# Where the gate weights of a piece stand among its w2 loads, and the gate units in front of the w2 steps, in the last stages of a one-layer Hymba-style kernel

## The reference

```
xn = RMSNorm(x);  z = xn @ W_in                       # RG-LRU heads and attention heads, then W_out, residual
h  = h + HierMoE(RMSNorm(h))                          # top group of 4, top 2 of its 8 experts, 32 experts in all
         expert e: (silu(t @ w1[e]) * (t @ w3[e])) @ w2[e],  w1, w3: 2048 x 512,  w2: 512 x 2048
pe   = RMSNorm(p @ W_ple)
gate = sigmoid(RMSNorm(h) @ w_pg + b_pg)              # w_pg: 2048 x 2048
out  = h + gate * pe
```

## Time and profile before

| | us |
|---|---|
| median of 3 runs (lowest, highest) | 1387.04 (1386.98, 1390.51) |
| the profiled execution | 1388.14 |
| its span, first to last instruction | 1386.1 |
| TensorE busy in the span | 1089.3 (79%) |
| mean granted TensorE clock | 0.900 of full |

### The profile page before, as it was taken

The page is one execution under the profiler, slowest core; times in us unless marked ns, Lnnn a source line. Parts: engine busy times, 40 slices in busy tenths (PEclk is TensorE's granted clock), DMA queues, the critical chain, the costliest instruction groups (busy, mean ns, idle before and its releaser), DMA issues.

```text
span 1386.1 us, 13825 instructions
## 1 busy us (share of the span) xinstructions
PE 1089.3 (79%) x6016; PEld 504.8 (36%) x6016; DVE 285.3 (21%) x439; ACT 156.7 (11%) x314; POOL 53.4 (4%) x66
## 2 busy tenths in 40 slices
PE   8999999999876686666765667666576656989998
PEld 4458887445522232222222223222232212333333
DVE  1104726412321212121221121000000000111116
ACT  1111315002200011000000000000000000010102
POOL 0112110200000002000000000000000000000000
PEclk9999999999888899788898788888888877999999
DMA  9943334354599999999999999999999999999961
GB/s 351 305 152 122 122 122 147 129 217 182 227 426 426 429 426 427 429 426 428 429 426 428 428 426 426 415 427 428 414 427 415 427 428 409 384 395 387 397 267 61
DMA packets 91053, 476.14 MB, mean 344 GB/s; under 512 B 10272, under 2 KB 10416, under 8 KB 67952
## 3 DMA queue, kind: packets, MB, share of 16 engines
q1 hardware_dynamic: 84896, 471.88, 84.1%
q0 software_dynamic: 560, 2.88, 0.6%
q10 hardware_dynamic: 5536, 0.47, 0.3%
HBM read 473.12 MB, written 2.10 MB: 343 GB/s over the span
## 4 chain that ended last, share of the span: by engine, by line
DMA 50%; PE 47%; SPq 1%; DVE 1%; issue 1%; ACT 0%; DVEq 0%
DMA ring<-in_w 48%; PE ps L1421 8%; PE ps L1384 6%; PE ps L1851 6%; PE ps L1674 5%; PE ps L1754 4%; PE ps L1545 4%; PE ps L1558 4%; PE ps L1809 2%; DMA area<-in_w 2%; PE ps L1646 2%; PE ps L1822 1%; PE ps L1639 1%; SPq L386 1%; PE ps L1578 1%
## 5 line engine op out<-in xcount | busy, mean ns | idle before, releaser
L1754 PE MATMUL ps<-ring,area 128*32 128x512 f32 x1024 | 166.4, 796 | 122.6 <-DMA ring<-in_w 122.0
L1674 PE MATMUL ps<-ring,area 128*32 128x512 f32 x976 | 147.7, 724 | 126.2 <-DMA ring<-in_w 126.2
L1184 DVE TENSOR_TENSOR h<-ps,h 128x2048 f32<-128x2048 f32 x32 | 73.3, 2292 | 298.8 <-PE ps L1646 298.8
L1754 PEld LDWEIGHTS ps<-ring,area 128*32 128x32 f32 x1024 | 43.1, 139 | 232.3 <-issue 232.3
L1421 PE MATMUL ps<-hT,ring 128*128 128x256 f32 x512 | 112.9, 380 | 0.0
L1674 PEld LDWEIGHTS ps<-ring,area 128*32 128x32 f32 x976 | 31.6, 122 | 222.7 <-issue 222.4
L1421 PEld LDWEIGHTS ps<-hT,ring 128*128 128x128 f32 x512 | 96.5, 190 | 14.0 <-issue 1.2
L1851 PE MATMUL ps<-ring,area 128*128 128x512 f32 x192 | 88.6, 603 | 6.3 <-DMA ring<-in_w_pg 4.9
L1384 PE MATMUL ps<-ring,hT 128*128 128x512 f32 x192 | 85.0, 602 | 1.1 <-DVE hT L907 1.1
L1229 DVE TENSOR_TENSOR hT<-area,ps 128x128 f32<-128x128 f32 x16 | 4.6, 288 | 315.8 <-ACT area L860 315.8
L1639 PE MATMUL ps<-area,hs 128*128 128x128 f32 x512 | 66.2, 284 | 0.5 <-DVE area L1165 0.5
(11 more groups left out here) (278 smaller groups left out, 775.0 us busy)
## 6 DMA issues: line engine op xcount, KB each, us to landing
ring<-in_w SPq DMA_DIRECT2D x157, 2048.0 KB, 21.5
ring<-in_w SPq DMA_DIRECT2D x57, 1024.0 KB, 15.1
ring<-in_w_in SPq DMA_DIRECT2D x28, 1024.0 KB, 12.6
ring<-in_w_out SPq DMA_DIRECT2D x16, 1024.0 KB, 7.2
ring<-in_w_pg SPq DMA_DIRECT2D x12, 1024.0 KB, 15.7
area<-in_w SPq DMA_DIRECT2D x2, 2048.0 KB, 14.0
hs<-in_w SPq DMA_DIRECT2D x4, 1024.0 KB, 14.3
hs<-in_w_pg SPq DMA_DIRECT2D x3, 1024.0 KB, 17.4
```

The source lines that it names most:

```text
L1184: dve.tensor_tensor(h[:, t, :], ps[:, bank:bank + 4, :].rearrange("p b n -> p (b n)"), h[:, t, :], ALU.add).then_inc(acc_done, 1)
L1674: ins = mm(ps[SLOTS * g:SLOTS * g + SLOTS, 0, :], XG[:, b, k, SLOTS * e:SLOTS * e + SLOTS], s[:, D_EXP * kk:D_EXP * kk + D_EXP], start=(k ...
L1754: ins = mm(ps[SLOTS * g:SLOTS * g + SLOTS, 0, :], XG[:, b, k, SLOTS * e:SLOTS * e + SLOTS], s[:, D_EXP * kk:D_EXP * kk + D_EXP], start=(k ...
```

## The change

The four `w_pg` chunks of piece i are loaded in front of the last quad of w2 of the same piece i (piece 0's stand first of all, piece 3's last of all, as before). In each of the three stages two gate units of the piece before stand in front of each w2 step, so that all eight are done in front of the last w2 step. VectorE adds all eight in front of `add_piece`. The counts of used chunks follow the new order.

```diff
 def w2_used(i, q, k):
     if i == 0:
         return QUAD_CHUNKS * q + 4 * W13_CHUNKS + k + 1
-    return OPEN_CHUNKS + 20 * (i - 1) + 4 * q + k + 1
+    behind_gate = 4 if q == OPEN_QUADS - 1 else 0
+    return OPEN_CHUNKS + (4 * OPEN_QUADS + 4) * (i - 1) + 4 * q + behind_gate + k + 1
 def w_pg_used(i, kk):
-    return OPEN_CHUNKS + 20 * i + 16 + kk + 1
+    return OPEN_CHUNKS + (4 * OPEN_QUADS + 4) * i + 4 * (OPEN_QUADS - 1) + kk + 1
+def gate_units(q):
+    return range(-(-8 * q // OPEN_QUADS), -(-8 * (q + 1) // OPEN_QUADS))
 def piece_loads():
-    order = []
+    order = [("w_pg", 0, kk, 0) for kk in range(4)]
     for i in range(1, PIECES):
         w2_ = [("w2", i, q, k) for q in range(OPEN_QUADS) for k in range(4)]
-        w_pg_ = [("w_pg", i - 1, kk, 0) for kk in range(4)]
-        order += w_pg_ + w2_ if i == 1 else w2_[:4] + w_pg_ + w2_[4:]
-    return order + [("w_pg", PIECES - 1, kk, 0) for kk in range(4)]
+        w_pg_ = [("w_pg", i, kk, 0) for kk in range(4)]
+        order += w2_ + w_pg_ if i == PIECES - 1 else w2_[:-4] + w_pg_ + w2_[-4:]
+    return order
...
             for i in range(PIECES):
                 if i:
-                    for u in range(7):
+                    for u in range(2 * 4):
                         add_gate(i - 1, u)
                 add_piece(i)
-                if i:
-                    add_gate(i - 1, 7)
                 copy_turned(i)
...
             for i in range(1, PIECES):
                 for q in range(OPEN_QUADS):
-                    if i > 1:
-                        w2_piece(i, q)
-                        if q:
-                            scatter_piece(i, q - 1)
-                    gate_unit(i - 1, 2 * q)
-                    if q < OPEN_QUADS - 1:
-                        gate_unit(i - 1, 2 * q + 1)
-                    if i == 1:
-                        w2_piece(i, q)
-                        if q:
-                            scatter_piece(i, q - 1)
+                    for u in gate_units(q):
+                        gate_unit(i - 1, u)
+                    w2_piece(i, q)
+                    if q:
+                        scatter_piece(i, q - 1)
                 scatter_piece(i, OPEN_QUADS - 1)
-                gate_unit(i - 1, 7)
                 turn_piece(i)
```

## The result

The changed kernel takes 1391.49 us (median of 22 runs, 1390.25 to 1397.27) against 1388.97 of the kernel before (22 runs, 1385.93 to 1390.98). The ratio is 1.0028, with an interval of 1.0019 to 1.0037: a quarter of a per cent slower, or 3.9 us. It weighs all executions and isn't the quotient of the two medians, which is 1.0018. Fifteen of the 22 times lie between 1390.2 and 1391.9, two at 1393.7 and 1393.9, and five between 1396.0 and 1397.3. The profiled execution, 1397.27 us with a span of 1394.9, is the slowest of the 22, which will matter.

A forecast was written before the change was run, and what follows sets the result against it. The piece stages were read as a race between a full load stream and TensorE, nearly balanced. Piece 3's units at 1353.0 against 1352.0, plus 2.5 clock, less 0.3 tail: +3.2, taken as +3.0; median 1390.0 us, range 1385.0 to 1394.5.

The forecast's parts named there:

- The late last quad: Piece 1's last w2 quad: loads 21 to 24 land 10 us later than before, at 1237.4; scatters end at 1243.6.
- The hand-off: Last scatter to next piece's gate units: adds and turn no longer covered, 3.56 us at each of three hand-offs.
- Start of piece 1's units: First gate unit of piece 1: 1243.6 plus a hand-off of 3.56, so it starts at 1247.2.
- No load is late behind it: Behind piece 1's last quad: all load waits go, 6.8 + 2.5 us; load 44 is 0.3 late at worst.
- The clock at hand-offs: Behind the three bare hand-offs: half of three clock falls of 1.7 us each, 2.5 us; ends 0 and 5.1.
- rival A: The clock falls at every hand-off: 1.0 + 5.1 = +6 us, 1393, slower; chance 0.27.
- the row of piece 0: Profile row of the kernel before: clock fell to 0.50 behind piece 0's turn for 3.3 us; evidence for falls.
- The sum: Whole span: 1353.0 + 2.5 - 1352.0 - 0.3 = +3.2, taken as +3.0 us; median 1390.0 us, 0.22% more.
- The terms without falls: The sum's part without clock loss at hand-offs: piece 3's units at 1353.0 against 1352.0, and 0.3 off the tail.
- The bound below: Were w2 (1, 3) not late, load 44 sets piece 2's units at 1298.8, piece 3's at 1351.7: -0.3 us.
- The split between the two prices: How the forecast loss divides between piece 1's late w2 quad and the bare hand-offs, whose clock loss was put at 2.5 us.

The follow-up runs named there:

- e7: The changed kernel run again with no edit, on another chip; ratio to the kernel before 1.0035, median 1395.63 us.
- e1: The changed kernel, but w_pg of piece 1 loaded behind the last quad of piece 1's w2 instead of in front; ratio to the kernel before 1.0027.
- e9: The changed kernel with each piece's w_pg loaded behind all of its own w2, hand-offs bare; ratio to the kernel before 0.9979.
- e6: The changed kernel with each piece's w_pg behind all of its own w2 and unused filling matmuls at the hand-offs; ratio to the kernel before 0.9958.
- e2: The kernel before with only the load order of the change, TensorE's order left as it was; ratio to the kernel before 1.003.
- e4: The kernel before, load order untouched, with three gate units instead of two ahead of the second w2 step for pieces 2 and 3; ratio 0.9966.
- e3: The changed kernel with three unused filling matmuls at each hand-off behind pieces 1 to 3; ratio to the kernel before 1.0017.
- e5: e4 plus four unused filling matmuls: three ahead of w_pg chunks in piece 1's first unit, one behind piece 3's turn; ratio to the kernel before 0.997.
- e8: e6, but unit 7 behind the last scatter replaces the two filling matmuls there; ratio to the kernel before 0.9945, 1380.24 us.

## Why the prediction was right, point by point

- *The late last quad.* Forecast: from load 8's landing 42.8 us to load 24's (1237.4 - 1194.6), the last chunk at half clock in 1.84. Measured: 42.3 and 1.94. The idle time there was 5.2 us instead of "some 7", as the last two chunks ran at half clock. The scatters: 4.4 forecast, 4.37 measured.
- *The hand-off.* 3.56 us forecast; measured 1.47 idle and 2.08 from turn to unit, three times.
- *Start of piece 1's units*: 52.6 us behind load 8 forecast, 52.1 measured (e7 52.2).
- *No load is late behind it.* Right. A stage and its hand-off were to be 52.9 at full clock; without the fall it is 53.2 (e1, from piece 2's first unit to piece 3's).
- *The clock at hand-offs.* Half of three falls, 2.5 us, was a guess between 0 and 5.1, and no profile shows it: three have all three falls (the change, e7, e9), one has none (e1). The profiled execution of the change is rival A: +5.4 us from load 8 on, +6.1 forecast for it. Of the difference 0.8 is the third fall, which costs 0.9 and not 1.7. The argument against A, 49 us of unbroken work ahead of the later hand-offs, didn't hold; nor does the argument for it, the row of piece 0, since in the change, e7 and e1 the same gaps at piece 0 kept the clock. What decides it stays open.
- *The sum.* +3.0 us forecast, +2.5 measured as the difference of the medians, 3.9 by the ratio; 1390.0 us against 1391.49. That it is so near is in part luck. The terms without falls give 1353.0 - 1352.0 - 0.3 = +0.7 (the text goes on with 1.0), and the profile of the change less its falls gives 5.4 - 4.3 = +1.1; what was measured over all executions lies above both, and why wasn't found. The times of before stand in two groups of eleven, and the median, 1388.97, falls in the gap between them. It moved by 1.9 us when it was taken over 22 runs instead of 3, and with it the absolute time.
- *What I had wrong in the argument.* The bound below, "were w2 (1, 3) not late at all, load 44 would set the end", names the right load for the change's own order: in e1 load 44 lands 96.0 us behind load 8, 96.1 forecast, and piece 2's units start 2.1 us later than the bound has them, as the chunks and scatters ahead run at half clock. But I read it as near the floor of the stage. It is not: load 44 is late because w_pg 2 was put ahead of it. The same fault stands twice in the change, and the second is hidden behind the first. e6 and e9 take both away.
- *The split between the two prices.* By that bound the late w2 (1, 3) was worth 1.3 us (1353.0 against 1351.7), and most of the +3.0 was charged to the clock at the hand-offs. The runs say that the places of w_pg cost more than the whole loss, some 7 us by e9 against the change, and that the new order of work goes with a gain once the loads suit it. The number came out right with this split wrong. The forecast of e2 failed on it too.

Not settled: why load 8 lands at 1194.6 to 1199.0 in different executions; when a bare hand-off loses the clock; and what makes the groups of times. The kernel before has two as well (1385.9 to 1388.0 and 1389.9 to 1391.0), and e1 has two, 1390.1 to 1390.4 and 1391.9 to 1393.1, with its profile without falls in the upper one. Falls of the clock and the landing of load 8, which alone varies by as much, are both possible causes; no execution of two groups of one kernel was profiled, so neither is shown.

## What to carry to other kernels

When transfers of a full queue are reordered, price the load that moves back and not only the one that comes early: find its consumer, see what else could run meanwhile, and then look whether the same move is made again further on, where the first stall hides it. An order of work and an order of loads have to be judged together: here the same order of work was 0.3% slower than before with one order of loads and 0.2% faster with another. Look first for work whose inputs are there: three gate units instead of two ahead of the second w2 step (e4) gained 0.3% with the loads untouched. In these runs filling saved time only where TensorE and not the stream was the bound (4 us in e3, nothing in e5).

## What the runs showed of the hardware that was not expected

Two gaps of 1.47 and 1.01 us with 1.06 us of transposes between them can take the granted clock to 0.50: behind pieces 1 to 3 they did so nine times out of nine in the change, e7 and e9, and not once in three in e1, and behind piece 0 (1.45 and 1.01 us) they left it at 1.00 in the change, e1, e7 and e8, and not in the kernel before, e2, e4 and e5. One gap of 1.01 left it at 1.00 in all three profiles that have it alone (before, e2 and e4, ahead of piece 3's units). The Trainium skill (TensorE: Matmul & The Clock Gate, section Why this matters for your kernels) names only a longer single gap; these rows differ from it, and they decide. Such a fall costs 1.7 us (8.80 against 7.10 for the same matmuls), but 0.9 in the last eight units. That three of them make the groups of times isn't shown. In e2, where four chunks arrived one by one and TensorE idled 0.7 to 0.8 us ahead of each of the last three, the clock stood at 0.52 over 14 us.
